# First norm of a two-layer trunk: GpSimd makes the first weight rests, tiles are normalised one ahead, and three unread products precede TensorE's sums

## The reference

```python
def _rms(x, eps=NORM_EPS):
    return (xf * lax.rsqrt(jnp.mean(xf * xf, axis=-1, keepdims=True) + eps)).astype(x.dtype)

def _modulate(h, shift, scale):
    return _rms(h) * (1.0 + scale) + shift

def _swiglu(h, w13, w2):
    a, b = jnp.split(h @ w13, 2, axis=-1)
    return (jax.nn.silu(a) * b) @ w2

ml = _split_mod(cond_lat @ mod_w[i] + mod_b[i])     # 9 vectors of 1024; ml[0] shift, ml[1] scale
h = h + 0.5 * ml[2] * _swiglu(_modulate(h, ml[0], ml[1]), ffn1_w13[i], ffn1_w2[i])
```

## Time and profile before

| | us |
|---|---|
| median of 3 executions | 1901.37 |
| lowest, highest | 1899.33, 1901.51 |
| the profiled execution | 1904.52 |
| its span in the profile | 1902.6 |

### The profile page before, as it was taken

One profiled execution on the slowest core, in us unless ns is written; L12 is line 12 of the kernel. 1 busy time (PEld: TensorE's weight loads), 2 busy tenths in 40 slices (PEclk: granted clock), 3 DMA queues, 4 the chain that ended last, 5 costly groups with the idle time before them and its releaser, 6 DMA issues.

```text
span 1902.6 us, 27442 instructions
## 1 busy us (share of the span) xinstructions
PE 1850.8 (97%) x9984; PEld 1587.8 (83%) x9984; DVE 1185.4 (62%) x1898; ACT 687.8 (36%) x1152; POOL 149.6 (8%) x228
## 2 busy tenths in 40 slices
PE   8999999999989999999999999999999989989997
PEld 6888888898966888888889888888898879978886
DVE  7877772355478478777424887752377445667764
ACT  5332232233258243223223322322254323545552
POOL 0010000100301200011001001000100000010000
PEclk9999999999999999999999999999999989999999
DMA  8466643334510246565233566533343213545554
GB/s 320 148 206 196 194 150 107 92 106 158 145 55 1 67 155 199 189 196 184 91 104 98 178 213 195 187 113 92 99 151 108 69 46 111 177 155 177 193 167 127
DMA packets 81886, 271.85 MB, mean 143 GB/s; under 512 B 9489, under 2 KB 14865, under 8 KB 81809
## 3 DMA queue, kind: packets, MB, share of 16 engines
q1 hardware_dynamic: 62354, 201.58, 32.4%
q0 software_dynamic: 19456, 69.22, 12.1%
HBM read 267.62 MB, written 1.05 MB: 141 GB/s over the span
## 4 chain that ended last, share of the span: by engine, by line
PE 90%; DVE 5%; issue 2%; ACT 2%; DMA 1%; SPq 0%; POOL 0%; POOLq 0%; DVEq 0%; ACTq 0%
PE pt L1429 19%; PE pt L1430 19%; PE pt L1432 19%; PE pt L1404 9%; PE pt L1403 4%; PE pt L1622 2%; PE pt L1839 2%; PE pt L1841 2%; PE pt L1840 2%; DVE wl L860 1%; PE pt L1502 1%; PE pt L1626 1%; PE pt L1566 1%; PE pt L1721 1%; PE pt L1568 1%
## 5 line engine op out<-in xcount | busy, mean ns | idle before, releaser
L860 DVE TENSOR_TENSOR wl<-raw,wh 128x1024 fp32r<-128x1024 f32 (+2 forms) x394 | 432.0, 1135 | 411.6 <-ACT wh L571 407.3
L1429 PE MATMUL pt<-xh,wh 128*128 128x512 f32 (+1 forms) x1312 | 496.5, 378 | 3.3 <-DVE wl L860 3.1
L1430 PE MATMUL pt<-xh,wl 128*128 128x512 f32 (+1 forms) x1312 | 495.2, 377 | 0.0
L1432 PE MATMUL pt<-xl,wh 128*128 128x512 f32 (+1 forms) x1312 | 493.8, 377 | 0.0
L571 ACT CAST wh<-raw 128x1024 fp32r<-128x1024 f32 (+2 forms) x394 | 364.2, 970 | 281.5 <-PE pt L1432 148.5
L872 DVE CUSTOM_DVE_ANT_0 pt<-modw,raw 128x1024 f32<-128x1024 f32 x256 | 305.7, 1253 | 17.4 <-DMA modw<-in_mod_rows 17.3
L1429 PEld LDWEIGHTS pt<-xh,wh 128*128 128x128 f32 x1312 | 248.4, 189 | 48.5 <-issue 3.7
L1432 PEld LDWEIGHTS pt<-xl,wh 128*128 128x128 f32 x1312 | 248.3, 189 | 45.5
L1430 PEld LDWEIGHTS pt<-xh,wl 128*128 128x128 f32 x1312 | 248.5, 189 | 44.6
L720 ACT CAST uh<-tmp 128x512 f32 (+3 forms) x88 | 49.7, 567 | 293.3 <-DVE tmp L1164 284.8
L1430 PE MATMUL pt<-uh,wl 128*128 128x512 f32 x396 | 154.1, 389 | 0.0
(11 more groups left out here) (222 smaller groups left out, 2782.5 us busy)
## 6 DMA issues: line engine op xcount, KB each, us to landing
raw<-in_ffn_w SPq DMA_DIRECT2D x238, 512.0 KB, 4.0
modw<-in_mod_rows POOLq DMA_DIRECT2D x128, 512.0 KB, 4.6
raw<-in_ret_w_in SPq DMA_DIRECT2D x48, 512.0 KB, 4.5
raw<-in_diff_w_in SPq DMA_DIRECT2D x24, 512.0 KB, 4.4
raw<-in_ffn_w SPq DMA_DIRECT2D x32, 256.0 KB, 3.9
raw<-in_ret_w_out SPq DMA_DIRECT2D x16, 512.0 KB, 4.4
region<-in_mod_rows SPq DMA_DIRECT2D x8, 512.0 KB, 14.6
region<-in_mod_start SPq DMA_DIRECT2D x8, 512.0 KB, 15.0
```

Source lines behind the costliest of these rows:

```text
L860: nc.vector.tensor_tensor(flat(wl[:, s, cut]), raw[:, raw_slot(late, s, p), 0:part_rows * CW], flat(wh[:, s, cut].bitcast(F32)), ALU.subtr ...
L1429: nc.tensor.matmul(bank, w_hi[:, k, cut], hi(k), start=a, stop=False)
L1430: nc.tensor.matmul(bank, w_lo[:, k, cut], hi(k), start=False, stop=False)
L1432: return nc.tensor.matmul(bank, w_hi[:, k, cut], lo(k), start=False, stop=b)
```

## The change

Line numbers of the diff are those of the kernel after for added lines.

```diff
@@ GpSimd's queue, behind root(0, ...)
+                    for p in range(2):
+                        for s in range(2):
+                            cut = slice(p * DT // 2, (p + 1) * DT // 2)
+                            pool.wait_ge(hi_ready, 2 * p + s + 1)
+                            nc.gpsimd.tensor_tensor(flat(wl[:, s, cut]), modw_slot[:, s] if p else raw[:, s, :],
+                                                    flat(wh[:, s, cut].bitcast(F32)), ALU.subtract).then_inc(lo_ready, 1)
+                    for p in range(2):
+                        half = slice(p * DT // 2, (p + 1) * DT // 2)
+                        pool.wait_ge(hi_ready, 5 + p)
+                        nc.gpsimd.tensor_tensor(flat(extra_lo[:, half]), raw[:, p, :], flat(extra_hi[:, half].bitcast(F32)),
+                                                ALU.subtract).then_inc(lo_ready, 1)
@@ ScalarE, the two extra pieces
-                            if k >= DT - 2:
-                                p = k - (DT - 2)
+                            if k in (DT - 3, DT - 2):
+                                p = k - (DT - 3)
@@ VectorE, the first norm (start_pieces and extra_rest are gone)
-                    start_pieces(0)
-                    start_products(1)
                     dve.wait_ge(bcast_ready, 1)
                     start_tile(0)
                     start_shift(0)
-                    for k in range(1, 3):
-                        start_tile(k)
+                    start_tile(1)
+                    start_products(1)
                     for k in range(1, DT):
                         start_shift(k)
                         start_lo(k - 1)
-                        if k == 3:
-                            start_pieces(1)
                         if k + 1 < DT:
+                            start_tile(k + 1)
                             start_products(k + 1)
-                        if k + 2 < DT:
-                            start_tile(k + 2)
-                        if k == DT - 1:
-                            extra_rest(0)
                     start_lo(DT - 1)
-                    extra_rest(1)
@@ VectorE, up
+                    if q0 == 0:
+                        dve.wait_ge(lo_ready, 6)
                     pair(0, False, unit_first=ph["units"] > 0)
@@ TensorE, start_products(d): the four products with wh first
+                p = d // (DT // 2)
+                pe.wait_ge(hi_ready, 2 * p + 2)
+                pe.wait_ge(x_hi_done, halves * (d + 1))
                 for s in range(2):
-                    pe.wait_ge(lo_ready, 2 * (d // (DT // 2)) + s + 1)
-                    if s == 0:
-                        pe.wait_ge(x_hi_done, halves * (d + 1))
                     for t in range(2):
                         cut, bank = slice(t * P, (t + 1) * P), pt[:, 2 * s + t, :]
                         nc.tensor.matmul(bank, wh[:, s, d, cut], xh[:, d, :], start=(d == 0), stop=False)
+                for s in range(2):
+                    pe.wait_ge(lo_ready, 2 * p + s + 1)
+                    for t in range(2):
+                        cut, bank = slice(t * P, (t + 1) * P), pt[:, 2 * s + t, :]
                         nc.tensor.matmul(bank, wl[:, s, d, cut], xh[:, d, :], start=False, stop=False)
@@ TensorE, ahead of the sums of squares
+            pe.wait_ge(x_landed[0], 16)
+            for n in range(3):
+                nc.tensor.matmul(pt[:, 5, 0:LAT], ones[:], hT[:, 0, 0:LAT], start=True, stop=True)
```

More of the change, by code:

```diff
@@ L861, in rest @@
                                             flat(wh[:, s, cut].bitcast(F32)), ALU.subtract).then_inc(lo_ready, 1)
-            def start_pieces(p):
-                for s in range(2):
-                    cut = slice(p * DT // 2, (p + 1) * DT // 2)
-                    dve.wait_ge(hi_ready, 2 * p + s + 1)
-                    nc.vector.tensor_tensor(flat(wl[:, s, cut]), modw_slot[:, s] if p else raw[:, s, :],
-                                            flat(wh[:, s, cut].bitcast(F32)), ALU.subtract).then_inc(lo_ready, 1)
             def column_sum(dst, weights, j, products):
```

5 lines of the change are left out of this document (removed).

## The result

The changed kernel took 1907.73 us (median of 13 runs, 1901.98 to 1909.48) against 1901.37 for the kernel before (13 runs, 1898.72 to 1904.71). The ratio is 1.0027, with a 95% interval of 1.0019 to 1.0034: slower by 0.27% (by the medians 6.4 us), where +0.07% and at most 1906.2 us had been forecast. The profiled execution after took 1909.48 with a span of 1907.5, which is 4.96 us more than the profiled one before.

The account below looks back on a forecast made before the run. TensorE, 97% busy, bounds the kernel; a shift of "up" carries to the end. Terms −1.0 + 0.2 + 3.3 plus the clock gave +0.9 or +2.5 against the median; +1.4 taken: 1902.8 us, range 1898.0 to 1906.2.

Parts of the forecast that it names:

- The start of the norm: Ahead of tile 0: first product at 23.2 us, 1.0 earlier; unread products cost nothing or 0.1; rests 1 and 2 covered.
- The duration of a rest: Weight rests on GpSimd: 2.40 us per 1024-column subtraction, bounds 1.9 and 2.6, against VectorE's 1.22.
- the 7% rival: GpSimd and VectorE hardly hold each other up in the norm: 3.85 us of stalls go, 1897.5 us; chance 7%.
- the walk: Engine turns through the norm's tiles: TensorE stalls 0.4, 1.1, 0.6 and 1.75 us, 3.85 against 0.58 before, so +3.3.
- The clock's part: 1.2 GHz stretches in the norm: one in most executions, worth 0 to 3.2 us, half taken, 1.6.
- slower by two whole stretches: Two stretches at 1.2 GHz in the norm, by the stalls of tiles 3 and 6: 1906 us; second rival, chance 16%.
- Tile 0 with its shift: Norm's first tile: starts longer before the clock's rise, +0.2 us.
- The choice between the baselines: Whole change against the median: +0.9 us if the median contains the profiled slow stretch whole, +2.5 if not; +1.4 taken.
- The rival of the lifted clock: Three unread products ahead of the sums lift sums, shifts and tile 0 to 2.4 GHz: 1901 us; chance 10%.
- The late fetches: Two fetches behind rest 6, out at 55.7 to 57 us instead of 38.2: even a 1 us wait is covered.

Follow-up runs that it names:

- experiment 4: Changed kernel without its three unread products ahead of the sums: 1907.27 us, ratio 1.0033 to the kernel before.
- experiment 5: Changed kernel with only rests 1 and 2 on GpSimd, rests 3 to 6 back on VectorE: 1899.47 us, ratio 0.9992 to the kernel before.
- experiment 6: Changed kernel with one added wait: GpSimd's rest 4 starts only once `xl` of tile 2 is made; 1904.86 us, ratio 1.0019.
- experiment 8: Changed kernel with ScalarE making the two-column small scale, its added constants set last in SBUF so no other tile moves: 1901.42 us, ratio 1.0006.
- Experiment 9: Changed kernel with five unread 256-column products added in TensorE's wait for `xl` of tile 2: 1903.32 us, ratio 1.0016.
- experiment 11: Changed kernel with eight unread products ahead of the sums instead of three: 1907.53 us, ratio 1.0036.
- experiments 2 and 3: Kernel before with all six rests on GpSimd: fetches behind rest 6, 1913.4 us, ratio 1.0067; fetches ahead of rests 5 and 6, 1905.65 us, ratio 1.0023.
- experiments 1 and 12: Changed kernel with all six rests back on VectorE: 1900.01 us, ratio 0.9998; kernel before with the three unread products added: 1902.44 us, ratio 1.0006.
- experiment 15: Changed kernel, only rests 1 and 2 on GpSimd, tile 0's products ahead of shift 1's, more unread products: 1903.28 us, ratio 1.001.
- experiments 7 and 8: Changed kernel with ScalarE making the small scale: added constants ahead of other SBUF tiles, 1907.39 us, ratio 1.0032; set last, 1901.42 us, ratio 1.0006.

## Why the prediction was wrong

**The start of the norm: right.** First product forecast at 23.2, seen at 23.02; the unread products ended at 12.8 instead of 12.3, pushed the sums back by 0.3, and moved the first product by 0.16 at most (experiment 4). Rests 1 and 2 were free (experiment 5).

**The duration of a rest: right.** 2.40 us was taken from the adds of 256 and 512 columns; six rests took 2.35 to 2.56. The two engines do hold each other, as the earlier trace rows had shown; the 7% rival that they hardly would is out.

**The step that failed is the walk, at "rest 3 then waits for a sum and runs 33.2 to 35.6; the `xl` of tile 2 behind it is made 35.5 to 36.1".** The walk counts the small scale of two columns in with the sums and gives it no turn of its own. It is held like the two-tensor instructions: 2.22 us beside rest 3, 2.19 beside rest 1, 2.22 and 2.23 beside rests 5 and 6. So it, not `xl`, took the turn between rests 3 and 4; `xl` asked 0.1 us after rest 4 had begun and was held for the whole of it. Tile 2's stall was 2.4 and not 0.4, tile 3's none and not 1.1; tile 6 had 1.05 and not 1.75. Two runs show this cause: with the order of the walk put back by a wait (experiment 6) the stalls come where the walk has them, 0.29, 0.90, 0.36 and 1.04, and the ratio is 1.0019 instead of 1.0027, within the noise; with the small scale out of the way (experiment 8) it falls to 1.0006, clear of it. In the sum the stalls came to +3.8 and not +3.3, which is not much; their distribution mattered more, because of the clock.

The Trainium skill had the missing rule: its page SBUF — State Buffer, section Who interferes with whom, counts tensor-with-scalar instructions among those of VectorE that can take the port pair shared with GpSimd, where their operands allow it, beside those with two tensors in SBUF. By this rule the trace agrees, with 2.22 us against 0.23; the shift (L1017), which reads PSUM, took its 0.2 us everywhere. The prediction cited an earlier section of that page and took from it that a VectorE instruction with one input in SBUF stands outside the lock; it left out the other case named there, a mode in which such an instruction uses both ports.

**The clock's part: wrong in size, and the largest miss in the number.** Against the profiled execution before, the forecast was −1.0 + 0.2 + 3.3 − 1.6 = +0.9, and the budget is −1.15 + 1.37 + 3.8 + 1.5 = +5.5. Of the 4.6 us between them the clock's term has 3.1 (−1.6 forecast, +1.5 seen), tile 0 has 1.2 and the stalls 0.5; the first product gives 0.15 back. The forecast had one slow stretch worth 0 to 3.2 us. One stall of 2.4 us in tile 2 brought 10.3 us at the slow level, 4.7 us lost. Experiment 9 shows that the fall belongs to the idle time of this wait: with TensorE kept busy in it and nothing else changed, the clock stayed full, and 2.1 us by the ratios, 4.4 by the medians, came back without VectorE being any faster. That is between two fifths and two thirds of the loss (by the ratios the intervals of the two still overlap slightly). How long a fall lasts and whether a shorter wait brings one is not settled by it: experiment 8 had one with no such wait. The rival "slower by two whole stretches" (16%, 1906) was nearest in time, but it had the places wrong: one long stretch at tile 2 and none at tile 6. Tile 0 with its shift was a further miss, +1.37 where +0.2 had been taken: the rise of the clock came at 28.9 instead of 27.1, though the products had begun earlier. In the other kernels with a first product near 23 it came at 25.8 to 27.8, so this looks like a matter of the single execution.

**The choice between the baselines: wrong.** The text had +0.9 if the median before contains its slow stretch, +2.5 if it does not, and took +1.4 between them. It had itself seen that the profiled run was 3.15 above the median, as much as one stretch. The case that was worked out for that was +2.5, and it should have been the forecast, with a stretch of its own added where the walk had stalls: −1.0 + 0.2 + 3.3 + 3.2 = +5.7, which was the second rival's price and close to the measured +6.4 (by the medians; +5.1 by the ratio). The runs on record bear this out: of the 106 executions of the kernel before that ran beside the experiments, 7 had a mean granted clock of 0.987 or 0.988, as the profiled one had (0.987), and took 1904.26 to 1905.15 us; the other 99, at 0.989 to 0.992, took 1898.56 to 1902.9. So the profiled execution is of a rare kind, and its time was a poor base.

**The rival of the lifted clock** (10%): three products do not do it; eight do, from 14.3 to 21.0, but not as far as the first tile (experiment 11). The late fetches were priced rightly at nothing here, but with thin cover: where they went out at 65.0, as "up" began (65.2), they cost some 8 us (experiments 2 and 3); in after they went out at 63.2, 4.9 us ahead of "up".

Open are what makes the late stretches at half clock come in one execution and not in another, and how often the unprofiled runs of before and after had one in the norm. Their mean granted clock (before mostly 0.989 to 0.992, after 0.984 to 0.988 in ten of thirteen) says that after had more half-clock time, not where. It is a rough sign, as a run in which the clock rose early and fell again counts lower too: the profiled one of experiment 8 had 0.987 and took 1900.25 us.

## What to carry to other kernels

Before work is moved to GpSimd, list every VectorE instruction that will stand beside it, the two-column ones too, and walk the turns one by one: an instruction of 0.2 us can use up the turn on which the critical one depends. Where TensorE must wait for some 2 us, unread full-width products in the wait can give back as much as the wait itself is long, as they did here by keeping the clock up. Where a median and a profiled run differ by the price of one slow stretch, forecast from the case without it and add the stretches that the change brings. Within one kernel, the mean granted clock of each run helps to tell which kind the profiled one is.

## What the hardware showed that was not expected

- A VectorE instruction of two columns, one tensor in SBUF and scalars, took 2.18 to 2.24 us each of the 28 times (in 12 profiles) that it stood beside a GpSimd subtraction of 1024 columns; alone it takes 0.23.
- Behind eight unread products of 128x256 the full clock was granted from 14.2 us, while 7 us of one-row spread had not brought it. Behind three it came in one profile (experiment 8: 12.9 to 16.3) and not in the others. With eight it fell at 21.0, though TensorE had stood idle for only 0.63 us since 14.3; from 15.5 on it had run products of 1, 2 and 128 columns.
- 32 bytes per partition set ahead of the other tiles in SBUF made 512-column products in three untouched stages 6 ns longer (395 for 389). Which tile's address is to blame was not tried.
- An idle time of 2.4 us was followed by 3.4 to 10.2 us at half clock in all four kernels that had it. Below that there was no clean line: 0.58 us was followed by a fall in before and by none in experiments 1 and 12, 0.87 by one in experiment 15, 1.2 by one in experiments 2 and 3, and 1.04 by none in experiments 6 and 9. In experiments 7 and 8 a fall came with no wait of 0.1 us listed in the 9 us ahead of it.
